# Constant matmuls into an unread PSUM bank at five waits of TensorE

## The chip, the cores and the metric

One core of a Trainium2 chip runs the whole program in one launch. The metric is the device time of that launch in microseconds (us). The kernel before took 2173.15 us (median of 3 runs, 2167.86 to 2176.16 us).

## The reference, cut to what matters

Two blocks of two layers each run one after the other on a sequence of 256 tokens with 1024 features, all in float32.

```python
def first_block(x, ...):                       # "A" in the kernel
    for i in range(2):
        h = rmsnorm(x, norm1_g[i])
        mix = hybrid_mixer(h, w_in[i], ...)     # three attention mixers
        x = x + mix @ w_out[i]
        h = rmsnorm(x, norm2_g[i])
        x = x + conv_glu_ffn(h, w_up[i], conv_w[i], conv_b[i], w_down[i])
    return rmsnorm(x, final_g)

def second_block(x, c, ...):                   # "B" in the kernel
    for l in range(2):
        mod = (silu(c) @ ada_w[l] + ada_b[l]).reshape(1, 3, 3, 1024)
        y = swiglu(modulate(x, mod[:, 0, 0], mod[:, 0, 1]), ffn_w13[l, 0], ffn_w2[l, 0])
        x = layer_norm(ALPHA * x + 0.5 * (1 + mod[:, 0, 2]) * y, ...)
        y = token_mixer(modulate(x, mod[:, 1, 0], mod[:, 1, 1]), w_in[l], w_out[l], ...)
        x = layer_norm(ALPHA * x + (1 + mod[:, 1, 2]) * y, ...)
        y = swiglu(modulate(x, mod[:, 2, 0], mod[:, 2, 1]), ffn_w13[l, 1], ffn_w2[l, 1])
        x = layer_norm(ALPHA * x + 0.5 * (1 + mod[:, 2, 2]) * y, ...)
    return x
```

## The kernel before, in words

The residual stream `x` stays in SBUF as two tiles of 128 tokens by 1024 features. Each weight chunk of 128 x 2048 floats is loaded by a DMA of the SP queue into a ring of three buffers (`raw`). ScalarE copies it to a rounded high part (`hi`, line 1101) and VectorE subtracts to get the low part (`lo`, line 1487). TensorE multiplies high by high, high by low and low by high: `products` (lines 603 to 613), so every product is three matmuls. The order of the work is written out by hand in one program per engine. The engines meet on semaphores only.

TensorE (`pe`, lines 598 to 1082) runs a loop of two layers for block A and a loop of two layers for block B. The stages around the change are these.

- `to_features` (lines 615 to 627) turns `x` or its normed copy `xn` with 16 transposes (line 626) into the four banks `TP = ps[2:6]`. The fifth and later tiles wait until an earlier one has been read. ScalarE and VectorE then write the high and low features `hT_hi`, `hT_lo` (lines 1114 and 1504 in A, 1286, 1291, 1845 and 1850 in B).
- `ffn` (lines 652 to 695): the first tile `up(0)` waits for the features one by one. In B `gate_on_all` (line 645) follows, two matmuls of 128x512 in float32 with `const("ones")` as the weights. The down products gather in `ACC = ps[4:8]`.
- In A, four chunks of `w_out` are multiplied (line 831). TensorE then waits for the normed copy (line 833, `A["xn"]`), runs the second `to_features` and the ffn, and reaches the end of the layer (lines 836 and 837).
- In B, TensorE runs the first ffn (line 845), waits for the layer norm (line 846, `B["nx"]`), turns and multiplies `w_in`, runs the mixer and `w_out` (line 1077), waits for the second layer norm (line 1078) and runs the second ffn (line 1080). The end of the layer is at lines 1081 and 1082.

At the end of a layer of either block TensorE, ScalarE and VectorE each drain and add one to `layer_done` (lines 836, 1081, 1276, 1469, 1826, 2193). GpSimd waits until it is 3, clears it and the block's semaphores, and adds one to `layer_go` (lines 559 to 562 and 592 to 595). All three engines wait for that before they branch back.

During the waits of TensorE at the norms, VectorE adds the residual (lines 1809, 1824, and 1889 to 1898 with the statistics), and ScalarE or VectorE forms the norm (lines 1107 and 1109, 1499; 1311, 1926 and 1928; for the last norm of a B layer 1938 and 1944). The first feed-forward of every layer (both of A's, and the first of B's) also makes VectorE work on the modulation products of block B (line 1481), which are not part of the layer itself.

Of the kernel before, what the change touches and what calls it, by code (L numbers as in the profile page):

```python
# [215 lines left out]
def build(nc, t, only_first=False):  # L216

    with ExitStack() as ctx:
        def sb(name, shape, dt=F32):
            return ctx.enter_context(nc.sbuf_tensor(name, shape, dt))  # L220

        def sem(name):
            return ctx.enter_context(nc.semaphore(name))
# [10 lines left out]
        cst = sb("cst", [P, CONST.shape[1]])  # L234
# [106 lines left out]
        ps = [ctx.enter_context(nc.psum_tensor(f"bank{i}", [P, 512], F32)) for i in range(8)]  # L341
# [4 lines left out]
        def const(name, parts=P):  # L346
            a, w = CST[name]
            return cst[0:parts, a:a + w]
# [30 lines left out]
        start_in, small_in, out_st = sem("start_in"), sem("small_in"), sem("out_st")  # L379
# [35 lines left out]
        for n_ in (DIL_H, NSA_H, NSA_H, DSA_H):  # L415
            at_ = sum(n for _, n in GROUPS)
            GROUPS += [(at_, min(3, n_)), (at_ + 3, n_ - 3)]
        PLACE = [(g, k) for g, (_, n) in enumerate(GROUPS) for k in range(n)]
        OUT_W = TT * HD
        LAG_T, LAG_O, LAG_V = 2, 3, 4  # L420
# [178 lines left out]
        def _(pe):  # L599
# [3 lines left out]
            def products(out, pairs, features=None):  # L603


                n = len(pairs)
                for i, ((ah, al), (bh, bl)) in enumerate(pairs):
                    if features:
                        pe.wait_ge(features[0]["tp_lo"], features[1] * KT + i + 1)
                    nc.tensor.matmul(out, ah, bh, start=(i == 0), stop=False)  # L610
                    nc.tensor.matmul(out, ah, bl, start=False, stop=False)  # L611
                    last = nc.tensor.matmul(out, al, bh, start=False, stop=(i == n - 1))  # L612
                return last

            def to_features(N, v, src, modulated=False, order=range(KT)):

                for n, k in enumerate(order):
                    if n >= len(TP):
                        if modulated:
                            pe.wait_ge(*modulated_tile(v, n - len(TP)))  # L620
                        else:
                            pe.wait_ge(N["tp_lo"], v * KT + n - len(TP) + 1)
                    if k == 0 and n:
                        pe.wait_ge(N["mix"], 2)
                    for i in range(TT):
                        last = nc.tensor.transpose(TP[n % len(TP)][:, i * P:(i + 1) * P], src[:, i, k * P:(k + 1) * P], ident)  # L626
                    last.then_inc(N["tp"], 1)

            def token_chunk(out, slot, width, features=None):

                for i in range(TT):
                    rows = slice(i * P, (i + 1) * P)
                    last = products(out[:, i * width:(i + 1) * width],
                                    [((hT_hi[:, k, rows], hT_lo[:, k, rows]),
                                      (w_hi[:, slot, k * width:(k + 1) * width], w_lo[:, slot, k * width:(k + 1) * width]))
                                     for k in range(KT)], features if i == 0 else None)
                return last

            def feature_tile(out, slot, half, stride=2 * P, features=None):

                cols = lambda k: slice(k * stride + half * P, k * stride + half * P + P)
                return products(out, [((w_hi[:, slot, cols(k)], w_lo[:, slot, cols(k)]), (hT_hi[:, k, :], hT_lo[:, k, :]))
                                      for k in range(KT)], features)

            def gate_on_all(sub):

                pe.wait_ge(B["gdiag"], sub + 1)
                for half in range(2):
                    nc.tensor.matmul(GATE[half][:, :], const("ones"), gdiag[:, 4 * half:4 * half + 4, :].rearrange("p k n -> p (k n)"),
                                     start=True, stop=True).then_inc(B["gateb"], 1)  # L650

            def ffn(N, split, h0, v, gate=None):


                def up(f, f2, pos, slot, wait_bank=True, features=None):
                    pe.wait_ge(lo_done, pos + (1 + NEW) + split)
                    if wait_bank:
                        pe.wait_ge(N["h"], f + (h0 - 1))
                    feature_tile(UP[f2][:, 0:SEQ], slot, 0, features=features)
                    feature_tile(UP[f2][:, SEQ:2 * SEQ], slot, 1).then_inc(chunk_mm, 1)  # L660

                def down(f, f4, pos, slot, first=False, last_one=False):
                    pe.wait_ge(lo_done, pos + (1 + NEW) + split)

                    for k2, i in ((0, 0), (1, 0), (0, 1), (1, 1)) if last_one else ((0, 0), (0, 1), (1, 0), (1, 1)):
                        pe.wait_ge(N["hid_lo"], f + (h0 + k2 + 1))
                        rows = slice(i * P, (i + 1) * P)
                        for half in range(2):
                            cols = slice(k2 * DM + half * 512, k2 * DM + half * 512 + 512)
                            out = ACC[2 * i + half][:, :]  # L670
                            ah, al = hid_hi[:, f4 + k2, rows], hid_lo[:, f4 + k2, rows]
                            bh, bl = w_hi[:, slot, cols], w_lo[:, slot, cols]
                            nc.tensor.matmul(out, ah, bh, start=first and k2 == 0, stop=False, skip_group_check=True)  # L673
                            nc.tensor.matmul(out, ah, bl, start=False, stop=False, skip_group_check=True)  # L674
                            last = nc.tensor.matmul(out, al, bh, start=False, stop=last_one and k2 == 1, skip_group_check=True)  # L675
                        if last_one and (k2, i) == (1, 0):
                            last.then_inc(N["y0"], 1)
                    last.then_inc(chunk_mm, 1)

                def turn(j, first=False):  # L680

                    for r in range(2):
                        f, pos = j * 4 + 2 * r, j * 6 + (1 + 3 * r)
                        up(f + 1, 1, pos, 1, wait_bank=not (first and r == 0))
                        up(f + 2, 0, pos + 1, 2)
                        down(f, 2 * r, pos + 2, 0, first=first and r == 0)

                up(0, 0, 0, 0, wait_bank=False, features=(N, v))
                if gate is not None:
                    gate_on_all(gate)  # L690
                turn(0, first=True)
                with pe.Fori(1, (FT - 2) // 4) as j:
                    turn(j)
                up(FT - 1, 1, FFN_N - 2, (FFN_N - 2) % RING)
                down(FT - 2, 0, FFN_N - 1, (FFN_N - 1) % RING, last_one=True)

            with pe.Fori(0, DEPTH) as l:
# [30 lines left out]
                for h in range(IDX_H):  # L728
                    if h >= 2:
# [4 lines left out]
                                     start=True, stop=True).then_inc(A["ix"], 1)  # L734
# [92 lines left out]
                for c in range(A_WOUT):  # L827
# [2 lines left out]
                        pe.wait_ge(A["x"], c - 1)  # L830
                    token_chunk(G[c % 2], (A_WIN + c) % RING, GW, None if c else (A, 1)).then_inc(chunk_mm, 1)

                pe.wait_ge(A["xn"], 2 * TT)
                to_features(A, 2, xn)
                ffn(A, split + (A_WIN + A_WOUT), 0, 2)
                pe.drain().then_inc(layer_done, 1)
                pe.wait_ge(layer_go, l + 1)

# [3 lines left out]
            with pe.Fori(0, DEPTH) as l:  # L842
                split = l * B_N + S_A
                to_features(B, 0, x, modulated=True)
                ffn(B, split, 0, 0, gate=0)
                pe.wait_ge(B["nx"], TT)
                to_features(B, 1, x, modulated=True)

# [66 lines left out]
                for c, (ftiles, _, width) in enumerate(B_WIN):  # L915
                    s_ = B_S0["win"] + c
                    pe.wait_ge(lo_done, split + (s_ + 1 + NEW))
                    if c >= 2:
                        ftiles_b, _, width_b = B_WIN[c - 2]
# [154 lines left out]
                for c in range(B_WOUT):  # L1074
                    s_ = B_S0["wout"] + c
                    pe.wait_ge(lo_done, split + (s_ + 1 + NEW))
                    token_chunk(ACC[c][:, :], s_ % RING, GW).then_inc(chunk_mm, 1)
                pe.wait_ge(B["nx"], 2 * TT)
                to_features(B, 3, x, modulated=True)
                ffn(B, split + B_S0["ffn1"], FT, 3, gate=2)  # L1080
                pe.drain().then_inc(layer_done, 1)
                pe.wait_ge(layer_go, l + (DEPTH + 1))

# [1217 lines left out]
```

## Time and profile before

| what | value |
|---|---|
| median of 3 runs | 2173.15 us (2167.86 to 2176.16) |
| the profiled execution's own time | 2177.1 us |
| its span | 2175.4 us |
| mean granted clock of TensorE | 0.943 of full speed |
| TensorE matmuls, busy | 1975.5 us, 91% of the span |
| VectorE, busy | 1381.4 us, 64% |
| ScalarE, busy | 963.8 us, 44% |

The profile takes one execution. Its span runs from the first to the last recorded instruction, and 1.7 us of the execution's time lie outside it. Matmuls are pipelined: a row's duration reaches from the start of the matmul to its modelled end, so matmuls that follow each other overlap, and the distance between starts is what each one costs. PEclk is the granted clock: 1.00 is 2.4 GHz and 0.50 is 1.2 GHz. A fraction between them in a stretch means that the clock changed inside it.

### The profile page before, as it was taken

To read this page: it belongs to the slowest core of one execution; us is meant where nothing else is said; L and a number is where in the kernel's file an instruction comes from. 1 tells how busy PE (TensorE), PEld (TensorE's weight loads), DVE (VectorE), ACT (ScalarE), POOL (GpSimd) and SP (SyncE) were. 2 spreads that over 40 slices of the span, in tenths; PEclk is the share of its full clock that TensorE was granted. 3 is DMA by queue.
4 is the path that set the end of the run, shared out by engine and by line. 5 is a ranking of instruction groups with operands and counts; after the bars stand their busy time and mean duration, and the time that the engine had idled before them with its cause. 6 is when DMAs were issued, how large, how long until landed. Compare 5 with 4: busy or idle time off the path is not lost.

```text
span 2175.4 us, 36223 instructions
## 1 busy us (share of the span) xinstructions
PE 1975.5 (91%) x13906; PEld 1847.0 (85%) x13906; DVE 1381.4 (64%) x2155; ACT 963.8 (44%) x1479; POOL 147.4 (7%) x202
## 2 busy tenths in 40 slices
PE   7988999798899969998998989995999898898997
PEld 7878999797899959997887979995999788887996
DVE  4486788538677867667646565446776764746455
ACT  4455444445544444444544343433434545334432
POOL 0000000000000000002003320000000200512000
PEclk9998999889999989999998899997999999989999
DMA  7116676411577657863420145546776241024552
GB/s 270 44 57 253 248 301 250 142 62 59 189 286 286 255 214 285 302 230 120 147 92 1 59 138 192 192 156 237 268 279 226 101 167 57 1 97 154 178 190 78
DMA packets 54109, 373.22 MB, mean 172 GB/s; under 512 B 5984, under 2 KB 6880, under 8 KB 10848
## 3 DMA queue, kind: packets, MB, share of 16 engines
q1 hardware_dynamic: 51392, 361.45, 46.1%
q0 software_dynamic: 2016, 9.07, 1.2%
q8 instruction: 82, 1.34, 0.3%
q10 hardware_dynamic: 576, 0.99, 0.1%
q14 instruction: 43, 0.35, 0.1%
HBM read 370.45 MB, written 1.05 MB: 171 GB/s over the span
## 4 chain that ended last, share of the span: by engine, by line
PE 80%; DVE 12%; ACT 5%; issue 2%; DMA 1%; DVEq 0%; ACTq 0%; POOLq 0%; SPq 0%
PE bank L610 17%; PE bank L611 17%; PE bank L612 17%; PE bank L673 5%; PE bank L674 5%; PE bank L675 5%; DVE w_lo L1487 2%; PE bank L1030 2%; PE bank L1039 1%; PE bank L1038 1%; PE bank L626 1%; DVE scratch L1481 1%; ACT w_hi L1101 1%; DVE scratch L2042 1%; DVE scratch L1889 1%
## 5 line engine op out<-in xcount | busy, mean ns | idle before, releaser
L610 PE MATMUL bank<-hT_hi,w_hi 128*128 128x256 f32 x2432 | 702.6, 289 | 33.9 <-DVE scratch L1521 23.9
L1487 DVE TENSOR_TENSOR w_lo<-raw,w_hi 128x2048 fp32r<-128x2048 f32 (+2 forms) x270 | 618.4, 2292 | 139.5 <-ACT w_hi L1101 139.1
L611 PE MATMUL bank<-hT_lo,w_hi 128*128 128x256 f32 x2432 | 696.9, 287 | 0.0
L612 PE MATMUL bank<-hT_hi,w_lo 128*128 128x256 f32 x2432 | 696.3, 286 | 0.0
L1101 ACT ACTIVATE w_hi<-raw 128x2048 fp32r<-128x2048 f32 (+2 forms) x270 | 508.9, 1886 | 197.0 <-PE bank L675 120.1
L610 PEld LDWEIGHTS bank<-hT_hi,w_hi 128*128 128x128 f32 x2432 | 473.9, 195 | 41.8 <-DVE w_lo L1487 36.4
L611 PEld LDWEIGHTS bank<-hT_lo,w_hi 128*128 128x128 f32 x2432 | 473.7, 195 | 4.3 <-issue 1.4
L612 PEld LDWEIGHTS bank<-hT_hi,w_lo 128*128 128x128 f32 x2432 | 473.5, 195 | 0.5
L610 PE MATMUL bank<-w_hi,hT_hi 128*128 128x256 f32 (+2 forms) x800 | 234.7, 293 | 2.0 <-DVE hT_lo L1504 2.0
L611 PE MATMUL bank<-w_lo,hT_hi 128*128 128x256 f32 (+2 forms) x800 | 232.7, 291 | 0.0
L612 PE MATMUL bank<-w_hi,hT_lo 128*128 128x256 f32 (+2 forms) x800 | 232.4, 291 | 0.0
L673 PE MATMUL bank<-w_hi,hid_hi 128*128 128x512 f32 x528 | 207.1, 392 | 8.4 <-DVE hid_lo L1523 8.4
L674 PE MATMUL bank<-w_lo,hid_hi 128*128 128x512 f32 x528 | 206.4, 391 | 0.0
L675 PE MATMUL bank<-w_hi,hid_lo 128*128 128x512 f32 x528 | 205.5, 389 | 0.0
L1481 DVE SCALAR_TENSOR_TENSOR scratch<-scratch 128x1024 f32<-128x1024 f32 x144 | 171.1, 1220 | 11.6 <-ACT scratch L1095 11.6
L1131 ACT ACTIVATE scratch<-bank 128x256 f32<-128x256 f32 x88 | 33.7, 383 | 297.5 <-PE bank L612 297.2
L610 PEld LDWEIGHTS bank<-w_hi,hT_hi 128*128 128x128 f32 x800 | 161.2, 202 | 4.2 <-issue 4.1
L611 PEld LDWEIGHTS bank<-w_lo,hT_hi 128*128 128x128 f32 x800 | 161.1, 201 | 0.0
L612 PEld LDWEIGHTS bank<-w_hi,hT_lo 128*128 128x128 f32 x800 | 161.0, 201 | 0.0
L1523 DVE TENSOR_TENSOR hid_lo<-scratch,hid_hi 128x256 fp32r<-128x256 f32 x132 | 56.2, 426 | 157.7 <-ACT hid_hi L1137 157.7
L1521 DVE TENSOR_TENSOR scratch<-scratch,bank 128x256 f32<-128x256 f32 x132 | 55.3, 419 | 109.9 <-ACT scratch L1131 108.9
L673 PEld LDWEIGHTS bank<-w_hi,hid_hi 128*128 128x128 f32 x528 | 99.4, 188 | 29.7 <-DVE hid_lo L1523 11.0
(352 smaller groups left out, 2361.9 us busy)
## 6 DMA issues: line engine op xcount, KB each, us to landing
raw<-in_wb SPq DMA_DIRECT2D x168, 1024.0 KB, 5.0
raw<-in_wa SPq DMA_DIRECT2D x96, 1024.0 KB, 4.8
scratch<-in_wm SPq DMA_DIRECT2D x72, 1024.0 KB, 6.5
lnw<-in_ln_g POOLq DMA_DIRECT2D x6, 512.0 KB, 3.9
lnw<-in_ln_b POOLq DMA_DIRECT2D x6, 512.0 KB, 5.9
cst<-in_const POOLq DMA_DIRECT2D x1, 2205.0 KB, 9.4
raw<-in_wa SPq DMA_DIRECT2D x4, 512.0 KB, 3.5
scratch<-in_c SPq DMA_DIRECT2D x4, 512.0 KB, 4.4
```

Source lines behind the costliest of these rows:

```text
L610: nc.tensor.matmul(out, ah, bh, start=(i == 0), stop=False)
L611: nc.tensor.matmul(out, ah, bl, start=False, stop=False)
L612: last = nc.tensor.matmul(out, al, bh, start=False, stop=(i == n - 1))
L673: nc.tensor.matmul(out, ah, bh, start=first and k2 == 0, stop=False, skip_group_check=True)
L674: nc.tensor.matmul(out, ah, bl, start=False, stop=False, skip_group_check=True)
L675: last = nc.tensor.matmul(out, al, bh, start=False, stop=last_one and k2 == 1, skip_group_check=True)
L1030: nc.tensor.matmul(ps[n % 4][:, 0:P], atm[:, n % 4, :], xx[:, u, 0, :], start=True, stop=True).then_inc(B["y"], 1)
L1101: nc.scalar.activation(w_hi[:, slot, 0:width], raw[:, raw_slot, 0:width], ACT.Copy).then_inc(hi_done, 1)
L1481: return nc.vector.scalar_tensor_tensor(out=w, in0=w, scalar=1.0, in1=cb, op0=ALU.mult, op1=ALU.mult, accum_out=column)
L1487: nc.vector.tensor_tensor(w_lo[:, slot, 0:width], raw[:, raw_slot, 0:width], w_hi[:, slot, 0:width].bitcast(F32), ALU.subtract).then_inc(l ...
L1521: nc.vector.tensor_tensor(h32[:, f2, :], sg[:, f2, :], UP[f2][:, SEQ:2 * SEQ], ALU.mult).then_inc(N["h"], 1)
L1523: nc.vector.tensor_tensor(hid_lo[:, f4, :], h32[:, f2, :], hid_hi[:, f4, :].bitcast(F32), ALU.subtract).then_inc(N["hid_lo"], 1)
```

## The change

A helper issues `n` matmuls of `const("ones")` (128 x 128) with the first 512 columns of the constants, in float32, into the bank `ps[3]`. Nothing waits for them and nothing reads what they write: at all five places the next writer of `ps[3]` is the `to_features` that follows on the same engine. It is called with 4 before the second norm of an A layer (together with a wait for the load of the constants), with 5 at the end of an A layer, with 6 before the first and with 6 before the second layer norm of a B layer, and with 10 at the end of a B layer. At the ends of the layers the calls stand ahead of the drain that adds to `layer_done`.

```diff
+            def keep_busy(n):
+
+                for _ in range(n):
+                    nc.tensor.matmul(ps[3][:, :], const("ones"), cst[:, 0:512], start=True, stop=True)
+
@@ block A, after the four chunks of w_out
+                pe.wait_ge(start_in, 32)
+                keep_busy(4)
                 pe.wait_ge(A["xn"], 2 * TT)
                 to_features(A, 2, xn)
                 ffn(A, split + (A_WIN + A_WOUT), 0, 2)
+                keep_busy(5)
                 pe.drain().then_inc(layer_done, 1)
                 pe.wait_ge(layer_go, l + 1)
@@ block B, after the first ffn
                 ffn(B, split, 0, 0, gate=0)
+                keep_busy(6)
                 pe.wait_ge(B["nx"], TT)
@@ block B, after the four chunks of w_out
+                keep_busy(6)
                 pe.wait_ge(B["nx"], 2 * TT)
                 to_features(B, 3, x, modulated=True)
                 ffn(B, split + B_S0["ffn1"], FT, 3, gate=2)
+                keep_busy(10)
                 pe.drain().then_inc(layer_done, 1)
                 pe.wait_ge(layer_go, l + (DEPTH + 1))
```

## Rows read from the trace of the kernel before

**Rows 1.** The page: the span, and the busy time of the engines.

```profile
span 2175.4 us, 36223 instructions
PE 1975.5 (91%) x13906; PEld 1847.0 (85%) x13906; DVE 1381.4 (64%) x2155; ACT 963.8 (44%) x1479; POOL 147.4 (7%) x202
```

**Rows 2.** The page: the chain that ended last, by engine.

```profile
PE 80%; DVE 12%; ACT 5%; issue 2%; DMA 1%; DVEq 0%; ACTq 0%; POOLq 0%; SPq 0%
```

**Rows 3.** The waits of TensorE: us in total, times, longest us.

```profile
PE bank L626 <- DVE x L1928: 27.4, 4, 7.5
```

**Rows 4.** The chain of waits, 991 to 1024 us: start us, us, what.

```profile
1009.71 0.12 PE bank L612
1009.82 1.72 PE bank L649 x4
```

**Rows 5.** Timeline at the second norm of A, both layers: start us, us, what.

```profile
194.72 3.74 PE L626 MATMUL bank<-cst,scratch 128*128 128x128 f32 x16 [4.89 <-DVE scratch L1499]
195.45 3.53 ACT L1114 ACTIVATE hT_hi<-bank,spa 128x256 fp32r<-128x256 f32 x8 [2.43 <-PE bank L626]
...
584.37 3.50 PE L626 MATMUL bank<-cst,scratch 128*128 128x128 f32 x16 [4.89 <-DVE scratch L1499]
584.84 3.53 ACT L1114 ACTIVATE hT_hi<-bank,spa 128x256 fp32r<-128x256 f32 x8 [2.18 <-PE bank L626]
```

**Rows 6.** The chain of waits after it, 186 to 216 us.

```profile
201.61 6.95 DVE scratch L1481 x12
```

**Rows 7.** Timeline at the ends of A's two layers.

```profile
391.19 0.39 PE L675 MATMUL bank<-w_hi,hid_lo 128*128 128x512 f32 x1
...
394.12 0.20 ACT L1109 ACTIVATE st<-st 128x2 f32<-128x2 f32 x1
...
399.78 1.97 PE L626 MATMUL bank<-cst,scratch 128*128 128x128 f32 x8 [8.20 <-DVE scratch L1499]
...
780.57 0.39 PE L675 MATMUL bank<-w_hi,hid_lo 128*128 128x512 f32 x1
...
783.50 0.20 ACT L1109 ACTIVATE st<-st 128x2 f32<-128x2 f32 x1
...
784.36 0.17 DVE L1493 RECIPROCAL st<-st 128x2 f32<-128x2 f32 x1 [2.08 <-POOLq L561]
```

**Rows 8.** Timeline at the first layer norm of B's first layer.

```profile
1002.49 3.67 PE L626 MATMUL bank<-cst,x 128*128 128x128 f32 x16 [7.47 <-DVE x L1928]
...
1007.36 1.08 DVE L1850 TENSOR_TENSOR hT_lo<-scratch,hT_hi 128x256 fp32r<-128x256 f32 x3
...
1009.66 1.88 PE L649 MATMUL bank<-scratch,cst 128*128 128x512 f32 x4
```

**Rows 9.** Timeline at the second layer norm of B, both layers.

```profile
1270.72 3.64 PE L626 MATMUL bank<-cst,x 128*128 128x128 f32 x16 [6.23 <-DVE x L1928]
...
1964.12 3.40 PE L626 MATMUL bank<-cst,x 128*128 128x128 f32 x16 [6.23 <-DVE x L1928]
```

**Rows 10.** Timeline between B's two layers.

```profile
1468.05 0.39 PE L675 MATMUL bank<-w_hi,hid_lo 128*128 128x512 f32 x1
...
1476.37 2.48 DVE L1944 SCALAR_TENSOR_TENSOR x<-x,st,lnw 128x1024 f32<-128x1024 f32 x2
...
1483.61 2.77 PE L626 MATMUL bank<-cst,x 128*128 128x128 f32 x10 [15.18 <-issue]
```

**Rows 11.** Stretches: from:to, length, busy of PE, PEld, DVE, ACT, POOL, then PEclk.

```profile
212.00:214.00 2.00, 1.85 (x10) 1.88 (x11) 1.00 (x4) 1.91 (x3) 0.00 (x0) 0.66 0.99 369
...
392.00:394.00 2.00, 0.00 (x0) 0.00 (x0) 0.90 (x2) 1.06 (x2) 0.00 (x0) 0.89 0.00 0
...
1176.00:1218.00 42.00, 41.95 (x374) 41.65 (x372) 34.27 (x79) 19.15 (x68) 32.16 (x64) 1.00 0.01 2
...
1966.00:1968.00 2.00, 2.00 (x15) 2.00 (x14) 2.00 (x6) 2.00 (x7) 0.00 (x0) 0.72 0.00 0
```

**Rows 12.** Timeline in the ffn of A's first layer.

```profile
212.15 0.35 PE L610 MATMUL bank<-hT_hi,w_hi 128*128 128x256 f32 x1 [1.90 <-DVE scratch L1521]
```

## The prediction

> **What bounds the kernel now.** I read the page first. TensorE is busy for 91% of the 2175.4 us [rows 1], and the mean granted clock is 0.943. The chain that ended last is on TensorE for 80% and on VectorE for 12% [rows 2]. So the kernel is bound by TensorE with short stretches that belong to VectorE, and the reader should see that the norms are such stretches: TensorE stands idle and VectorE and ScalarE work. The waits of TensorE say how long. The two layer norms inside B's layers cost 27.4 us in four waits [rows 3], two of 7.47 us and two of 6.23 us [rows 8, 9]. The second norm of an A layer costs 4.89 us, twice [rows 5]. The hand-over between A's layers costs 8.20 us [rows 7] and the one between B's layers 15.18 us [rows 10]. The change can shorten none of these waits, since in each TensorE waits for others. It can only change the clock at which TensorE works behind them, and it can make TensorE late. I then read the timeline at each place for these two things, and the stretches for the clock.
>
> **What one constant matmul costs.** Line 649 is the same shape (128x512, float32, constants as weights or as data). Two of them are four instructions and take 1.72 us on the chain at full clock [rows 4], so one takes 0.86 us, and at half clock it would take 1.72 us. The fills last 4 x 0.86 = 3.44, 5 x 0.86 = 4.30, 6 x 0.86 = 5.16 and 10 x 0.86 = 8.60 us. The wait for the constants' load costs nothing: it was issued at the start and a first mixer lies between.
>
> **Where the fill makes TensorE late.** At the norms each fill is shorter than its wait: 3.44 of 4.89, 5.16 of 7.47, 5.16 of 6.23 us [rows 5, 8, 9]. They leave 1.45, 2.31 and 1.07 us idle and cost nothing as long as the clock is full. Between B's layers the last down product ends at 1468.05 + 0.39 = 1468.44, the fill would end at 1477.04, and VectorE's norm ends at 1476.37 + 2.48 = 1478.85 [rows 10]. The fill is covered with 1.8 us to spare, and what comes back later is every engine's branch, not TensorE. The last layer is the same.
>
> The ends of A's layers are different. The hand-over needs all three engines. TensorE's last product ends at 391.58, the fill ends at 395.88, but ScalarE, which is the last to report today, ends at 394.32 [rows 7]. The third report comes 1.56 us later. In the second layer it is 780.96 + 4.30 = 785.26 against 783.70, again 1.56 us [rows 7]. Behind that report lies GpSimd's clearing and then everything: 784.36 is VectorE's reciprocal, released by line 561 and only 0.66 us after ScalarE's end [rows 7]. SP's loads for the next ffn part, ScalarE's load of the layer's small parameters and VectorE's norm all wait for `layer_go`. Nothing covers this. Cost: 2 x 1.56 = 3.1 us. From below it could be nothing, if the drain lets TensorE report while the fill is in flight, which no row shows; from above it is the full length of both fills, 2 x 4.30 = 8.6 us. I take 3.1.
>
> **What the clock gives back.** The clock fell at the ends and norms today: in 392 to 394 us it is 0.89, and TensorE had been idle since 391.58 [rows 7, 11]. If 0.89 is full clock and then half, it fell 0.44 us before 394, at 393.56, that is 1.98 us after TensorE stopped.
>
> *Second norm of A.* Only the start of the features is on the chain. Today the high features start 195.45 - 194.72 = 0.73 us behind the first transpose in the first layer. In the second, where the transposes started at a higher clock, it is 584.84 - 584.37 = 0.47 us [rows 5]. So 0.26 us is to be had, once. The rest of what TensorE gains goes into a wait: VectorE works 6.95 us on the modulation products behind the features, on the chain [rows 6], and TensorE waits for it until 212.15 [rows 12]. 0.26 us.
>
> *First layer norm of B.* Here 16 transposes, then the 24 products for the gates, then line 649 stand on the chain. The products can't end before the last feature, 1007.36 + 1.08 = 1008.44 [rows 8], which a full clock makes 0.26 earlier, and three products of 0.12 us each [rows 4] must follow it: 1008.18 + 0.36 = 1008.54 against the start of line 649 at 1009.66. At most 1.12 us each. But will the clock be full? After the fill there are 2.31 us of idleness and then transposes that wait for each other. In the ffn of A TensorE was idle for 1.90 us before 212.15, and the clock in 212 to 214 us is 0.66, so it fell just behind that wait [rows 11, 12]. 2.31 is longer. I take half: 0.56 each, 1.1 together, with 0 and 2.2 as ends.
>
> *Second layer norm of B.* The idle rest is only 1.07 us, so I expect the clock to hold. But today's half clock covers only the transposes: they start at 1964.12 and in 1966 to 1968 us the clock is already 0.72, so it rose inside that stretch [rows 9, 11]. The features set the pace of the products; the gain is their earlier start, 0.26 us each, 0.5 together, with 0 and 1.0 as ends.
>
> *The ends of the layers.* After the fill TensorE is idle from 395.88 to the shifted start of the transposes, 399.78 + 1.56 = 401.34, 5.5 us, and between B's layers from 1477.04 to 1483.61, 6.6 us [rows 7, 10]. Both are far above the 1.98 us after which the clock fell. The clock will be half when the work resumes, as today. No gain. In B the ten matmuls buy nothing at all.
>
> Here a rule of the Trainium skill speaks against the change. The rows show a clock that rose while TensorE had done nothing but transposes since its idle wait: they began at 1964.12 and last 3.40 us, and 1966 to 1968 us stands at 0.72 [rows 9, 11]. The page "TensorE: Matmul & The Clock Gate", in its part "PE-mode transpose", says that transposes don't count as TensorE being busy in the same way and don't bring the full clock. By that rule the clock would fall in the transposes behind every fill, the first layer norm would give 0 in place of 1.1, and the sum would be 1.1 us higher. The trace disagrees with it here, and I go by the trace.
>
> **The sum.** +3.1 - 0.26 - 1.1 - 0.5 = +1.2 us. The profiled execution took 2177.1 us (2175.4 of span and 1.7 around it), so the same execution would take 2178.3. It lies 4.0 us above the median of the runs, 2173.15, and the difference carries over: 2174.4 us. From the terms' ends: the least is 0 - 0.26 - 2.2 - 1.0 = -3.5 us, the most +8.6.
>
> **The rivals.**
>
> *A: the fill holds the clock at every norm and the drain lets the report through early.* For it: the rests of 1.07 to 2.31 us are about as short as waits that TensorE has everywhere. Against it: the 1.90 us wait of rows 12, and a drain that would have to ignore what it drains. Result -3.5 us, 2169.7. If only the clock holds and the late report stays, it is -0.4 us, 2172.8.
>
> *B: the change does nothing.* The clock falls behind all the fills, and the hand-over is late for another reason. Result 0 to +0.3, 2173.2. For it speaks that the mean clock is 0.943, so most of each layer runs at full clock already. Against it stand the plain times of rows 7.
>
> *C, the other side: the constants don't keep the clock, and the fill runs at half clock and outlasts its waits.* Say the clock falls 1.98 us into every fill, as in an idle wait. Then 2.3 matmuls are done and the rest take 1.72 us each. The fill of 5 takes 1.98 + 2.7 x 1.72 = 6.6 us and reports 3.9 us late, twice: 7.8. The fill of 6 takes 8.3 us: 0.9 longer than 7.47, twice 1.7; 2.1 longer than 6.23, twice 4.2. The fill of 10 takes 15.2 us and ends at 1483.7, 4.8 behind VectorE. The fill of 4 takes 4.9 us and just fits. Sum +18.5, 2191.7 us. It passes 0.5% once about three fifths of this extra is real. Against it: in 1176 to 1218 us float32 matmuls fill TensorE and the clock is 1.00 throughout [rows 11]. For it only that ones and constants are unlike data, which no row tests alone.
>
> **How the numbers follow.** The forecast, late reports at A's ends and small gains at the norms, has a chance of 0.62. A has 0.16, B 0.14, C 0.05; 0.03 stay for something unnamed. Three runs of the same kernel spread over 8.3 us, so no less than 0.5% (10.9 us) can be told from no change. The spread of the runs is wider than my terms' ends. Around 2174.4 I add about half of it on each side to the cases of A, B and the forecast: 2166 to 2183 us, which leaves out C and the far ends. Faster by over 0.5% means below 2162.3, and no case reaches it: 0.04. Slower by over 0.5% means above 2184.0, which is C and part of the unnamed: 0.07. Within: 0.89.
>
> **What would show it.** The new matmuls stand 0.43 us apart per instruction, all at full clock (C is wrong). GpSimd's line 551 starts about 4.3 + 0.3 us after TensorE's last product of A's first layer in place of ScalarE's end, so VectorE's reciprocal in the next layer comes 1.6 us later against the down products (or the cost term is wrong). The clock in the transposes of the second layer norm of B is 1.00, in those of the first it is mixed. From the first transpose to line 649 the first layer norm takes 6.1 to 7.2 us in place of 1009.66 - 1002.49 = 7.17. The stretches behind the ends of the layers stay at 0.50. The prediction is wrong if the median moves by more than the spread of the runs, or if the ends of A come no later and the norms give over 1 us each.

## The result and the profile after

| | before | after |
|---|---|---|
| median of 20 runs each | 2171.68 us (2164.49 to 2179.96) | 2178.84 us (2173.42 to 2185.67) |
| ratio of after to before, 95% interval | | 1.0027 [1.0016, 1.0038] |
| the profiled execution's own time | 2177.1 us | 2178.43 us |
| its mean granted clock | 0.943 | 0.959 |

The ratio is +5.9 us (3.5 to 8.3) of 2172. (The two medians alone differ by 7.2 us.) The forecast was 1.2 us over the kernel before, a median between 2166 and 2183 us, and no difference of more than 0.5%. The last two held, and the change costs some 5 us more than the sum says. Two things have to be found: which terms were wrong, and where the excess is.

The page of the kernel after: the span, and the busy time of the engines. It answers to [rows 1].

```profile
span 2176.7 us, 36471 instructions
PE 2020.0 (93%) x14030; PEld 1857.9 (85%) x14030; DVE 1382.0 (63%) x2155; ACT 963.8 (44%) x1479; POOL 147.3 (7%) x202
```

TensorE has 124 more matmul instructions: 62 products of two instructions each. TensorE is busier by 44.5 us, its clock is higher, and the span is no shorter: both numbers look better, and neither is the time.

The waits of TensorE in the kernel after (us in total, times, longest us), beside [rows 3], and from the costliest groups the row of the fill.

```profile
PE bank L626 <- DVE x L1939: 6.9, 4, 2.4
```

```profile
L648 PE MATMUL bank<-cst 128*128 128x512 f32 x124 | 54.8, 592 | 0.0
```

The wait at B's norms went from 27.4 to 6.9 us, since the fill stands in it. The norms take as long as before.

**The ends of A's layers.** Timeline of the kernel after at the end of A's first and second layer (start us, us, engine line op out<-in xcount [idle before <-releaser]), beside [rows 7].

```profile
393.05 0.39 PE L680 MATMUL bank<-w_hi,hid_lo 128*128 128x512 f32 x1
393.27 4.45 PE L648 MATMUL bank<-cst 128*128 128x512 f32 x10
...
395.97 0.20 ACT L1120 ACTIVATE st<-st 128x2 f32<-128x2 f32 x1
...
398.54 0.90 POOL L551 MEMSET gateb<- 128x960 f32 x1 [308.06 <-PEq L844]
...
401.37 0.17 DVE L1504 RECIPROCAL st<-st 128x2 f32<-128x2 f32 x1 [6.61 <-issue]
...
403.04 1.97 PE L626 MATMUL bank<-cst,scratch 128*128 128x128 f32 x8 [5.31 <-DVE scratch L1510]
...
780.07 4.45 PE L648 MATMUL bank<-cst 128*128 128x512 f32 x10
...
782.76 0.20 ACT L1120 ACTIVATE st<-st 128x2 f32<-128x2 f32 x1
...
785.17 0.17 DVE L1504 RECIPROCAL st<-st 128x2 f32<-128x2 f32 x1 [3.62 <-POOLq L561]
```

The fill ends at 397.72, 1.55 us behind ScalarE's 396.17, and GpSimd's memset behind the clearing (line 551) now names TensorE's drain (line 844) as its releaser. Measured from the last product, VectorE's reciprocal came at +6.53 us before (398.11 - 391.58) and comes at +7.93 us (401.37 - 393.44). From VectorE's first down residual to its first operation of the next norm it was 9.43 us in the first layer and 6.28 in the second; it is 10.81 and 7.83: +1.38 and +1.55. These two numbers are the "distances" below.

**The first layer norm of B.** Timeline of the kernel after, first layer, beside [rows 8].

```profile
996.40 5.31 PE L648 MATMUL bank<-cst 128*128 128x512 f32 x12
1004.09 1.82 PE L626 MATMUL bank<-cst,x 128*128 128x128 f32 x12 [2.38 <-DVE x L1939]
1006.15 0.90 PE L626 MATMUL bank<-cst,x 128*128 128x128 f32 x4 [0.24 <-ACT scratch L1297]
...
1010.25 1.88 PE L654 MATMUL bank<-scratch,cst 128*128 128x512 f32 x4
```

Stretches of the kernel after (from:to, length, busy of PE, PEld, DVE, ACT, POOL, then PEclk and two columns on DMA): the hand-over behind A's first layer, the first layer norm of B, the hand-over between B's layers, and the second layer norm of B.

```profile
403.00:405.00 2.00, 1.96 (x8) 1.57 (x8) 1.17 (x1) 1.95 (x4) 0.00 (x0) 0.50 0.12 41
...
1002.00:1004.00 2.00, 0.00 (x0) 0.00 (x0) 1.69 (x4) 0.20 (x1) 0.00 (x0) 1.00 0.00 0
1004.00:1006.00 2.00, 1.76 (x12) 1.26 (x12) 0.90 (x3) 1.34 (x4) 0.00 (x0) 1.00 0.00 0
1006.00:1008.00 2.00, 1.83 (x13) 1.28 (x13) 2.00 (x7) 2.00 (x7) 0.00 (x0) 1.00 0.00 0
...
1484.00:1488.00 4.00, 1.25 (x5) 0.71 (x4) 4.00 (x6) 2.32 (x6) 0.00 (x0) 0.50 1.01 403
...
1966.00:1968.00 2.00, 1.69 (x14) 1.20 (x12) 1.22 (x3) 1.69 (x5) 0.00 (x0) 1.00 0.00 0
```

The clock held at full through the idle rest (2.38 us in the first layer, 2.33 in the second) and the transposes behind the first norm, and in both layers behind the second (1.00 where [rows 11] had 0.72). It did not hold behind the layers' ends: 0.50, as said. From the first transpose to line 654 the first norm takes 1010.25 - 1004.09 = 6.16 us in place of 7.17 [rows 8]: the gates' product (line 649 before, 654 after) comes 1.0 us earlier, nearly all of the 1.12 that the prediction gave as the most and twice what it took. So by its own profile the change should have come out better than forecast, and it came out worse.

### The profile page after: what moved, and what is told of

It is laid out like the page before. It is cut to its first block, busy times and chain, and to the rows that moved or that the text cites. A ratio compares the mean times of both kernels' runs of the same rounds, so it can differ in the third digit from the quotient of the medians.

```text
span 2176.7 us, 36471 instructions
## 1 busy us (share of the span) xinstructions
PE 2020.0 (93%) x14030; PEld 1857.9 (85%) x14030; DVE 1382.0 (63%) x2155; ACT 963.8 (44%) x1479; POOL 147.3 (7%) x202
## 4 chain that ended last, share of the span: by engine, by line
PE 78%; DVE 12%; ACT 5%; issue 2%; DMA 1%; PEldq 1%; PEld 0%; DVEq 0%; ACTq 0%; POOLq 0%; SPq 0%
PE bank L610 17%; PE bank L612 17%; PE bank L611 17%; PE bank L678 5%; PE bank L679 5%; PE bank L680 5%; DVE w_lo L1498 2%; PE bank L1039 2%; PE bank L1048 1%; PE bank L1047 1%; DVE scratch L1492 1%; PE bank L626 1%; ACT w_hi L1112 1%; DVE scratch L2053 1%; DVE scratch L1900 1%
## 5 line engine op out<-in xcount | busy, mean ns | idle before, releaser
L610 PE MATMUL bank<-hT_hi,w_hi 128*128 128x256 f32 x2432 | 699.2, 288 | 35.5 <-DVE scratch L1532 23.7
```

## The experiments

All were run in 12 executions each (the one with 20 products in 6), beside 29 to 35 executions of the kernel before on the same chip. A range in brackets is a 95% interval. The first four take the change apart.

**The fills at the norms alone.** Against the kernel after, the calls with 5 and 10 are left out.

```diff
                 ffn(A, split + (A_WIN + A_WOUT), 0, 2)
-                keep_busy(5)
...
                 ffn(B, split + B_S0["ffn1"], FT, 3, gate=2)
-                keep_busy(10)
```

> Fills only at the four norms (4, 6 and 6), none at the ends of the layers. Theory 1, the late reports at A's ends are what the change costs and the norms give back a little: 0.5 to 3 us faster than the kernel before, and the segment from the last down product of A to the next norm as before (9.4 and 6.3 us). Rival 2, fills at the norms cost something that the profile hides (the clock falls elsewhere, or the bank is contended): 2 to 4 us slower than before. Rival 3, the fills between B's layers cost: as theory 1.

Measured: 1.0009 [0.9992, 1.0027], +2.0 us (-1.7 to +5.9). In its trace the stretches at the norms are short as in the kernel after (7.77 and 7.75 us from the first norm's output to the gates' product, 10.76 twice at the second). The time shows none of it.

**The fill at A's ends alone.** Against the kernel before:

```diff
                 ffn(A, split + (A_WIN + A_WOUT), 0, 2)
+                keep_busy(5)
                 pe.drain().then_inc(layer_done, 1)
```

> Fills only at the ends of A's two layers (5 each). Theory 1: 3.1 us slower than before (1.56 us per end), the hand-over of A 1.4 to 1.6 us longer twice, no cold stretch less behind it. Rival 2: the same 3.1 or less, with the rest of the 6 us at the norms. Rival 3: 3.1.

Measured: 1.0025 [1.0010, 1.0040], +5.4 us (2.2 to 8.7). The distances are 10.89 and 7.85 us, +1.46 and +1.57. GpSimd's row in this trace:

```profile
399.43 0.90 POOL L551 MEMSET gateb<- 128x960 f32 x1 [308.94 <-PEq L842]
```

**The fill at B's ends alone.** Against the kernel before:

```diff
                 ffn(B, split + B_S0["ffn1"], FT, 3, gate=2)
+                keep_busy(10)
                 pe.drain().then_inc(layer_done, 1)
```

> Fills only at the ends of B's two layers (10 each). Theory 1: no difference from before, within 1 us; the fill ends 1.8 us ahead of VectorE. Rival 3, TensorE's drain or its branch back is late although the products are done, so the hand-over between B's layers or the end of the program is longer: 2 to 5 us slower.

Measured: 0.9994 [0.9979, 1.0009], -1.3 us (-4.6 to +2.0). From the first down residual to the last step of the layer's last norm (line 1944) it is 10.55 us with and without a fill, and from there to the next layer's first copy 7.09 against 7.31. Ten products there are free and useless.

**The whole change, with the ends' fills behind the report.**

```diff
-                keep_busy(5)
                 pe.drain().then_inc(layer_done, 1)
+                keep_busy(5)
                 pe.wait_ge(layer_go, l + 1)
```

and the same for the 10 of B.

> All fills of the change, but those at the ends of the layers stand behind the drain that reports, ahead of the wait for layer_go. Theory 1: as e1, 0.5 to 3 us faster than before, the hand-overs as before; in the wait for layer_go the fill of 5 ends 1.4 us behind the release but the branch back of the other engines takes 2.9 us and hides it. Rival 2: 2 to 4 us slower than before. Rival: the fill makes TensorE's branch back late, so the hand-over is longer by up to 1.5 us twice although the report is early.

Measured: 1.0014 [1.0001, 1.0027], +3.0 us (0.2 to 5.9). Timeline at the end of A's first layer in this kernel:

```profile
388.89 4.55 PE L648 MATMUL bank<-cst 128*128 128x512 f32 x10
...
391.32 0.20 ACT L1120 ACTIVATE st<-st 128x2 f32<-128x2 f32 x1
...
392.35 0.90 POOL L551 MEMSET gateb<- 128x960 f32 x1 [305.34 <-ACTq L1287]
```

GpSimd starts while the fill still runs, and ScalarE releases it. The second distance is back at 6.29 us. The first is 10.04, but for another reason: the layer's last down products ran partly at the lower clock, so VectorE's residual on the second 128 tokens starts 3.56 us behind that on the first in place of 2.74. From its start to the next norm it is 6.48 us, against 6.69 in the kernel before and 8.09 in the kernel after. So the lateness is the report's, not that of the products as such; the whole is lower than the change by 2.9 us, with intervals that overlap.

The parts sum to the whole (2.0 + 5.4 - 1.3 = 6.1 against 5.9). Of the three only A's ends are clear of zero, so they are where to look for the loss, and no gain of the norms is seen.

The next eight put weight on each part.

**Twenty products at A's ends.** Against the kernel before:

```diff
                 ffn(A, split + (A_WIN + A_WOUT), 0, 2)
+                keep_busy(20)
                 pe.drain().then_inc(layer_done, 1)
```

> Only the fill at A's two layer ends, with 20 products in place of 5. 20 products at the 0.43 us that the fill's profile showed are 8.6 us of TensorE; less the 0.6 us that the fill of 5 (2.15 us) lost before it was seen in the distance from the last residual to the next norm (+1.4 and +1.55 us), the report is 8.0 us late at each end. Theory 1, every microsecond of a late report is paid once and the rest of the +6 us that the fill of 5 cost is the scatter of where the half clock falls: the two distances grow to 17.4 and 14.3 us, and the time by +16 us (13 to 19). Rival, the price of a late report is a multiple of what the distance shows, as the fill of 5 had it (6.2 against 2.9 us): about +33 us. Rival, a fixed extra of some 3 us comes with any fill at these ends: about +19 us.

The expectation has an error that the row shows: one product is two instructions of 0.43 us, so 20 last twice as long as it says.

```profile
393.25 17.33 PE L648 MATMUL bank<-cst 128*128 128x512 f32 x40
...
411.40 0.90 POOL L551 MEMSET gateb<- 128x960 f32 x1 [320.80 <-PEq L842]
```

With the right length, 17.33 less the 2.9 us that are covered, theory 1 says 14.4 us at each end, 28.8 in all. Measured: distances of 23.71 and 22.31 us, +14.3 and +16.0; of the 16.0, 1.6 us lie ahead of the fill, in down products at the lower clock, so the second report is 14.4 us late and the two together 28.7. The time is 1.0117 [1.0090, 1.0145], +25.4 us (19.6 to 31.5). The expectation's numbers missed; the rule behind them, each microsecond of a late report once, stands. The rival of a price twice as high, put right in the same way, would be some 60 us, and is out.

**Three products at A's ends.** The same edit with `keep_busy(3)`.

> Only the fill at A's two layer ends, with 3 products in place of 5. The fill of 5 took 4.45 us and made the report 1.4 to 1.55 us late, so 2.9 to 3.05 us of it lie beside the last residual and ScalarE's sums; the fill of 3 takes 2.67 us and ends 0.3 us ahead of ScalarE. Theory 1: GpSimd starts behind ScalarE, not TensorE, the distances to the next norm are 9.2 to 9.4 and 6.28 us as without a fill, and the time is the same, 0 us with 1.5 us of scatter. Rival, a fill at these ends costs some 3 us beyond what it does to the report (the fill of 5 alone came out at +6): the same distances, but +3 us.

Measured: 1.0001 [0.9984, 1.0018], +0.2 us (-3.5 to +3.9); distances 9.20 and 6.31 us.

```profile
386.54 2.73 PE L648 MATMUL bank<-cst 128*128 128x512 f32 x6
...
389.24 0.20 ACT L1115 ACTIVATE st<-st 128x2 f32<-128x2 f32 x1
...
390.27 0.90 POOL L551 MEMSET gateb<- 128x960 f32 x1 [302.78 <-ACTq L1282]
```

The fill ends 0.17 us ahead of ScalarE's 389.44, and ScalarE is the releaser again. With 3, 5 and 20 products alone at A's ends the first distance is 9.2, 10.9 and 23.7 us: a threshold at ScalarE's end and a slope of one behind it (12.8 us more for 12.9 us more of fill).

**The whole change with 3 in place of 5 at A's ends.** Against the kernel after:

```diff
-                keep_busy(5)
+                keep_busy(3)
```

> The whole change, with fills of 3 in place of 5 at A's two layer ends. Theory 1: the late reports are gone, 2.9 us of the change's +5.9 us: +3.0 us against the kernel before (+0.5 to +5.5). Rival, the late reports are all of the loss: -1 to 0 us. Rival, they are none of it: +6 us.

Measured: 0.9994 [0.9975, 1.0013], -1.3 us (-5.4 to +2.8). The number fits the first rival, in which the late reports are all of the loss, better than theory 1; the intervals don't exclude theory 1. This is the version that loses nothing, and it is not faster than the kernel before.

**The fill at B's first layer norm alone.** Against the kernel before:

```diff
                 ffn(B, split, 0, 0, gate=0)
+                keep_busy(6)
                 pe.wait_ge(B["nx"], TT)
```

> Only the fill of 6 at B's first layer norm, in both layers. Theory 1: the clock is held through the transposes, the stretch from the norm's first output to the first gate product is 7.76 us in place of 8.8 in both layers, and nothing behind it depends on that: -2.0 us (-0.5 to -3.5 with the scatter). Rival, what the held clock gives at the norm is given back in the products behind it, since the half clock falls elsewhere: the same stretches of 7.76 us, but 0 to +1.5 us in the time.

Measured: 1.0001 [0.9984, 1.0019], +0.2 us (-3.5 to +4.1). The stretch to the gates' product is 7.76 and 7.75 us, as both said, and the time has nothing of the 2 us: by its middle the rival, though the interval doesn't exclude -2. The traces show the place. Timelines of the kernel before, then of this one, behind the first norm of B's first layer: GpSimd's two operations on `x` (line 579) and the memset behind them, VectorE's third split of the weights, and the product that waits for it.

```profile
1008.60 13.49 POOL L579 TENSOR_TENSOR x<-x,lnw 128x2048 f32<-128x2048 f32 x2 [219.81 <-DVE hT_lo L1850]
1022.03 1.88 POOL L584 MEMSET scratch<- 64x768 f32 x3
...
1020.79 3.45 DVE L1487 TENSOR_TENSOR w_lo<-raw,w_hi 128x2048 fp32r<-128x2048 f32 x1
...
1024.30 0.39 PE L610 MATMUL bank<-hT_hi,w_hi 128*128 128x256 f32 x1 [0.84 <-DVE w_lo L1487]
```

```profile
1006.76 13.48 POOL L579 TENSOR_TENSOR x<-x,lnw 128x2048 f32<-128x2048 f32 x2 [218.91 <-DVE hT_lo L1856]
1020.18 1.88 POOL L584 MEMSET scratch<- 64x768 f32 x3
...
1018.39 4.01 DVE L1493 TENSOR_TENSOR w_lo<-raw,w_hi 128x2048 fp32r<-128x2048 f32 x1
...
1022.45 0.38 PE L610 MATMUL bank<-hT_hi,w_hi 128*128 128x256 f32 x1 [1.41 <-DVE w_lo L1493]
```

Count from the norm's first output (1000.90 and 999.30). The gates' product comes at 8.76 and 7.76, 1.0 us earlier. VectorE's split starts at 19.89 and 19.09, 0.8 earlier, but takes 4.01 us in place of 3.45. TensorE goes on at 23.40 and 23.15, only 0.25 earlier: its wait grew from 0.84 to 1.41 us. What holds it is GpSimd's line 579, released by the last low feature, which comes only 0.25 us earlier with the full clock. TensorE goes on 2.27 us behind the memset that follows line 579 in both kernels (1024.30 - 1022.03 and 1022.45 - 1020.18), and 2.28 and 2.27 us in the second layers of the kernels before and after. A split with no GpSimd beside it, the next one of the kernel before, takes 2.29 us: the third makes next to no way while line 579 runs, however early it starts. The other kernels bear this out: in the 16 first norms without this fill the gates' product comes anywhere from 8.0 to 8.9 us behind the norm's first output and the third split starts at 19.3 to 20.0, and TensorE goes on at 23.39 to 23.41 in all of them; in the 12 with it the gates' product comes at 7.75 to 8.35, and TensorE goes on at 23.14 to 23.16. The chain of waits follows semaphores and so names, behind line 649 [rows 4], only the split, with 3.38 us where others take 2.29 (kernel before; start us, us, what):

```profile
1020.87 3.38 DVE w_lo L1487
```

That longer duration was the one sign in the kernel before that a gain at line 649 would not last. The Trainium skill names a cause that fits, page "SBUF — State Buffer", section "SBUF: two separate sides": a VectorE operation with two inputs in SBUF and a GpSimd operation that reads SBUF lock one pair of ports, each for its whole instruction, and the other waits. The split that waited and TensorE's return at 2.27 us behind GpSimd, about the length of one split, agree with it; no run here took GpSimd's operation away, so that it is this lock is not shown.

**The whole change without this fill.** Against the kernel after:

```diff
                 ffn(B, split, 0, 0, gate=0)
-                keep_busy(6)
```

> The whole change without the fill of 6 at B's first layer norm. In the profiles the gate products behind this norm came 1.0 us earlier with the fill, but 0.25 us were left of it 15 us later, where TensorE waits for VectorE's third split of the weights either way, and the stretch from this norm's first output to the next norm's was 267.95 us in the mean with the fill and 267.32 without. Theory 1, this fill gains nothing in the end: +4 to +6 us against the kernel before, the same as the whole change or a little less. Rival, its 1.0 us in each layer is a gain that stays: +8 us.

Measured: 1.0023 [1.0009, 1.0036], +5.0 us (2.0 to 7.8), against +5.9 with it. A gain of 2 us that stays would have left +8.

**The second norms alone.** Against the kernel before:

```diff
+                pe.wait_ge(start_in, 32)
+                keep_busy(4)
                 pe.wait_ge(A["xn"], 2 * TT)
...
+                keep_busy(6)
                 pe.wait_ge(B["nx"], 2 * TT)
```

> Only the fills at the second norm of A (4) and the second layer norm of B (6). Theory 1: -0.24 us at each of B's two, up to -0.56 at A's first and nothing at A's second: -0.5 to -1.0 us, not to be told from no change. Rival, one of these two places carries a hidden cost of some 3 us (the norms' three fills together came out at +1.3 us where their own stretches show -3): +2 to +3 us.

Measured: 0.9988 [0.9967, 1.0009], -2.6 us (-7.2 to +2.0). It could have been a gain, so the same code ran once more.

> Only the fills at A's second norm and at B's second layer norm once more, the same code as before, which came out at -3.6 us with an interval from -7.2 to +2. Theory 1, the stretches behind these norms are 0.25 us shorter in all four places and no more: -1.0 us, not to be told from no change. Rival, this part of the change is a gain of 3 us or more, and the version to keep: -3 us again.

Measured: 1.0016 [1.0002, 1.0031], +3.5 us (0.4 to 6.7). There is no gain of 3 us to keep. (The -3.6 in this expectation is the difference of the means; the ratio gives -2.6.) About the 1 us the pair is inconclusive, and it says more about the intervals: one code moved by 6 us between two sets, on two chips, so intervals of 3 to 5 us to a side look too narrow here. The norms' three fills ran twice too, the second time with no edit against the first.

> The fills at the norms alone once more, the same code as before, to narrow its interval, for 12 runs whose standard deviation is 5.6 us leave 1.6 us of doubt in their mean. Theory 1: its own stretches (-1.0 twice, -0.25 twice, -0.3 to -0.56 once) are all there is, the mean over both sets of runs comes out at -1 to -3 us, so this set at about -3. Rival, the gain is given back elsewhere: this set again at 0 to +2 us.

Measured: 1.0009 [0.9987, 1.0030], +2.0 us (-2.8 to +6.5), after +2.0 (-1.7 to +5.9). The middles of both sets stand with the rival, and neither shows a gain; but a gain of the 1.6 us that is found below still lies inside both intervals.

## Where the scatter is

The executions of one code spread over 6 to 19 us, and the traces show it before any fill has run: from A's first norm to the last residual of its mixer the fourteen kernels, whose instructions are the same so far, took 176.0 to 183.3 us. Stretches of the kernel with the fill at A's ends alone, which took 182.5 us there, and then of the one with the ends' fills behind the report, which took 176.0:

```profile
10.00:190.00 180.00, 162.72 (x1173) 151.29 (x1174) 106.60 (x248) 89.57 (x194) 6.40 (x11) 0.93 0.33 119
...
150.00:172.00 22.00, 19.37 (x104) 16.86 (x104) 14.45 (x36) 13.76 (x30) 0.00 (x0) 0.69 0.14 49
```

```profile
10.00:190.00 180.00, 162.86 (x1201) 149.31 (x1201) 107.60 (x250) 91.75 (x200) 6.42 (x11) 0.97 0.34 121
...
150.00:172.00 22.00, 18.60 (x131) 17.06 (x132) 14.02 (x29) 12.51 (x21) 0.00 (x0) 0.92 0.27 97
```

The same work, a mean clock of 0.93 and of 0.97, and in the one 22 us of products at 0.69 where the other has 0.92: 104 matmul instructions against 131. The clock falls at waits inside the mixers, in one execution here and in another there. The stretch from B's first to its second layer norm, start of output to start of output, took:

| fill at the first norm | layers | us, least to most | mean |
|---|---|---|---|
| with | 12 | 265.2 to 269.0 | 267.5 |
| without (the kernel before among them) | 16 | 265.5 to 270.9 | 267.4 |

So this stretch, gates' product included, is no shorter with the fill in the mean. In its quickest executions it is 265.2 and 265.3 with the fill and 265.5 in four layers without, about the 0.25 that GpSimd leaves. At the second norm the shorter time holds in all 16 layers that have the fill: 10.74 to 10.76 us to the gates' product, against 10.98 to 11.34 in the 12 without. Line 579 runs there too, and a split beside it takes up to 5.74 us, but the 0.25 us pass through: from this norm's first output to the layer's last down product it is 197.55 to 197.61 or 199.03 to 199.10 us with the fill, and 197.79 to 197.84 or 199.29 to 199.35 without. No run can show so little.

## Why the prediction was right, and what in it was wrong

- **A fill costs 0.86 us a product and runs at full clock.** Right: 4.45 us for 5 and 17.33 for 20. The rival with half clock in the fill is out: every fill of every kernel here ran at 1.00.
- **The report at A's ends comes 1.56 us late, twice.** Right in the trace: 1.38 and 1.55 us, 2.9 together, and the covered part was 2.9 us where I had 2.74. As a time, the fill alone measured +5.4 (2.2 to 8.7) and 20 products +25.4 (19.6 to 31.5) for 28.7 us of late reports, so the term stands within both intervals, and the multiple is out.
- **The drain might let the report through.** It doesn't: line 844's drain releases GpSimd, whose line 551 starts 0.8 us behind the fill's end. That is 5.1 us behind TensorE's last product, where the prediction's sign had 4.3 + 0.3; the 0.8 was there behind ScalarE before, so it adds nothing.
- **0.26 us at A's second norm, once.** A little too small, by the quick executions. There it is had in both layers: from the norm to the first down residual they took 194.12 to 194.15 us without and 193.57 to 193.90 with the fill, about 0.3 each. In the mean of all layers (16 with, 12 without) both are 194.7: in 10 of the 16 and 5 of the 12 the clock falls 18 to 20 us behind the norm, as it did at 212.65 us in the kernel before, and these layers take 1.2 to 2.0 us longer. Whether the fill makes that fall more frequent is not shown.
- **0.56 us at B's first norm, twice.** This step failed, in both of its halves. I halved the gain since the clock had fallen behind an idle 1.90 us in A's ffn; it held behind 2.32 to 2.38 us in 11 of the 12 layers with this fill. And I took line 649, which the chain shows, as the end of the reckoning. The path runs past it, from the last feature through VectorE's first splits, GpSimd's line 579 and the third split: of 1.0 us, 0.25 is left 15 us later. The term by the traces is -0.5 in place of -1.1.
- **0.26 us at B's second norm, twice.** Right, 0.25 each in the traces.
- **Nothing at the layers' ends.** Right: 0.50 behind them, and the ten products of B are covered.

With the terms as measured, the sum is 2.9 - 0.6 - 0.5 - 0.5 = +1.3 us, nearly the forecast, since the errors cancel, which is luck. It is luck too that the two profiled executions differ by 1.3 us: ahead of any fill, in A's first mixer, the one of the kernel after had already lost 2.7 us. And that the result lies within 0.5% says little for the sum, since 0.5% is 10.9 us. The measured +5.9 (3.5 to 8.3) is 4.6 us more than the 1.3. That the loss sits at A's ends is shown three times: by the fill alone, by 3 in its place (from +5.9 to -1.3) and by the slope. Over all sets, the three with 5 products ahead of the report have +5.9, +5.4 and +5.0 us, and the nine without a late report have -2.6 to +3.5, in the mean +0.6; the fills behind the report, at +3.0, are among the higher of these. That these ends cost more than the 2.9 us of their late reports is not shown: the 20 products cost 3 us less than their two late reports, and the rest is of the size by which two sets of one code differ. It could be that the delay moves where the half clock falls behind it; no stretch of the traces shows that, A's second mixer least (176.4 to 178.7 us in three kernels with the fill of 5 in front of the report, 174.6 to 181.5 in the others but that with 20, which took 175.9). This stays open.

The rule on transposes that the prediction weighed, of the Trainium skill's page "TensorE: Matmul & The Clock Gate", stood against the gain at the first norm. The traces go against it: the 16 transposes there ran at 1.00 in 11 of 12 layers with the fill, those at B's second norm in all 16. In one layer, of the kernel with the ends' fills behind, the clock fell inside them, with 2.38 us of idleness ahead as in layers where it held. Stretches of that kernel:

```profile
1688.00:1690.00 2.00, 1.01 (x8) 0.86 (x8) 1.17 (x3) 0.47 (x1) 0.00 (x0) 1.00 0.00 0
1690.00:1692.00 2.00, 1.69 (x10) 1.14 (x10) 1.73 (x5) 1.97 (x7) 0.00 (x0) 0.67 0.00 0
```

So the clock may fall behind such a wait and mostly doesn't, and the length of the wait alone doesn't say which.

## What to carry to other kernels

Work that fills a wait is free only up to the next report that others wait for: at a hand-over of several engines find the one that reports last, and keep the fill ahead of that moment or behind the report (5 products in front cost 2.9 us in the trace, 3 cost nothing). A higher clock behind a wait is worth what the next wait leaves of it, so follow the gain to the next instruction that another engine releases before it enters the sum. And where one code moves by 6 us from one set of runs to the next, read a change of 2 us in the stretches of the traces, not in the medians.

## What was not expected of the hardware

- The granted clock held at full through 2.32 to 2.38 us of idleness and 16 transposes in 11 of 12 layers, and fell behind 1.90 us in A's ffn [rows 11, 12]. Ahead of either wait TensorE had worked without a gap at 1.00: for 9.5 us on products and the fill in the kernel after (992.18 to 1001.71), for over 10 us on products ahead of the 1.90 (200.00 to 210.25). What tells the two apart is not shown.
- The third split of the weights beside GpSimd's `tensor_tensor` took 3.45 us where it started late and 4.01 where it started early, against 2.29 alone, and TensorE went on at the same 2.27 us behind GpSimd either way.
- Without any difference in code up to there, A's first mixer took between 176.0 and 183.3 us, a spread larger than the whole effect of the change.
